# Output norms scaled on VectorE through a PSUM bank, and weight remainders in two pieces, in a two-layer decoder step on one core

## The reference, cut to what matters

```
def rms_norm(x, g):
    y = x * rsqrt(mean(x * x, axis=-1) + EPS)
    return y * g

for i in range(2):
    h = rms_norm(x, norm_mix_pre[i])
    m = conformer_conv(h, ...) if i == 0 else mla(h, c_kv, k_rope, ...)
    x = x + rms_norm(m, norm_mix_post[i])
    h = rms_norm(x, norm_ff_pre[i])
    x = x + rms_norm(square(relu(h @ w_up[i])) @ w_down[i], norm_ff_post[i])
    x = x + sigmoid(x @ ple_gate[i]) * (ple[i] @ ple_proj[i])
```

## Time and profile before

| | us |
|---|---|
| median of 3 runs | 1917.44 |
| lowest and highest | 1915.46, 1927.88 |
| the profiled execution | 1916.53 |
| its span, from the first to the last instruction | 1914.4 |
| mean granted clock of TensorE in it | 0.96 of full |

### The profile page before, as it was taken

The page is one execution under the profiler, slowest core; times in us unless marked ns, Lnnn a source line. Parts: engine busy times, 40 slices in busy tenths (PEclk is TensorE's granted clock), DMA queues, the critical chain, the costliest instruction groups (busy, mean ns, idle before and its releaser), DMA issues.

```text
span 1914.4 us, 33398 instructions
## 1 busy us (share of the span) xinstructions
PE 1782.8 (93%) x12372; PEld 1605.6 (84%) x12372; DVE 920.4 (48%) x2169; ACT 737.9 (39%) x1457; POOL 1013.0 (53%) x737
## 2 busy tenths in 40 slices
PE   7987799989999999979899899999979999999978
PEld 6986799988999989879666465666969999999978
DVE  5896899844223256652444344442252222222383
ACT  5655444454444434432233333332332222223332
POOL 4993899967998975563111000001564555555562
PEclk9998899999999999989899899997979999999989
DMA  7331355533554523123003155555212222222201
GB/s 207 94 101 42 119 177 159 185 111 110 177 154 146 163 88 92 50 50 118 1 1 93 35 165 153 148 164 174 93 45 88 88 88 88 88 73 80 67 23 50
DMA packets 183289, 198.55 MB, mean 104 GB/s; under 512 B 32985, under 2 KB 138035, under 8 KB 183170
## 3 DMA queue, kind: packets, MB, share of 16 engines
q1 hardware_dynamic: 178414, 191.92, 32.4%
q10 hardware_dynamic: 4756, 5.04, 0.8%
HBM read 192.14 MB, written 4.79 MB: 103 GB/s over the span
## 4 chain that ended last, share of the span: by engine, by line
PE 71%; DVE 12%; POOL 10%; issue 3%; ACT 3%; DMA 1%; SPq 0%; ACTq 0%; POOLq 0%; DVEq 0%
PE bank L2340 18%; PE bank L2341 17%; PE bank L2342 17%; POOL WL L1328 6%; PE bank L2906 4%; PE bank L2940 3%; PE bank L2864 3%; DVE X L1657 2%; DVE AL L1625 2%; POOL acc L1354 1%; PE bank L2805 1%; DVE AL L1629 1%; PE bank L2786 1%; ACT WH L661 1%; POOL BL L1421 1%
## 5 line engine op out<-in xcount | busy, mean ns | idle before, releaser
L1328 POOL TENSOR_TENSOR WL<-RAW,WH 128x1024 fp32r<-128x1024 f32 (+1 forms) x281 | 666.2, 2380 | 678.5 <-ACT WH L661 676.7
L2340 PE MATMUL bank<-AH,WH 128*128 128x288 f32 x2112 | 646.0, 306 | 64.5 <-DVE AL L1625 31.3
L2341 PE MATMUL bank<-AL,WH 128*128 128x288 f32 x2112 | 633.6, 300 | 0.0
L2342 PE MATMUL bank<-AH,WL 128*128 128x288 f32 x2112 | 633.2, 300 | 0.0
L2340 PEld LDWEIGHTS bank<-AH,WH 128*128 128x128 f32 x2112 | 407.4, 193 | 80.0 <-DVE AL L1625 33.9
L2341 PEld LDWEIGHTS bank<-AL,WH 128*128 128x128 f32 x2112 | 407.9, 193 | 0.9
L2342 PEld LDWEIGHTS bank<-AH,WL 128*128 128x128 f32 x2112 | 407.3, 193 | 0.0
L661 ACT ACTIVATE WH<-RAW 128x1024 fp32r<-128x1024 f32 (+1 forms) x283 | 293.4, 1044 | 276.7 <-PE bank L2342 271.5
L2340 PE MATMUL bank<-BH,WH 128*128 128x288 f32 (+1 forms) x1120 | 337.7, 302 | 13.3 <-DVE S L1667 7.0
L2341 PE MATMUL bank<-BL,WH 128*128 128x288 f32 (+1 forms) x1120 | 334.8, 299 | 0.0
L2342 PE MATMUL bank<-BH,WL 128*128 128x288 f32 (+1 forms) x1120 | 334.6, 299 | 0.0
(11 more groups left out here) (271 smaller groups left out, 2128.8 us busy)
## 6 DMA issues: line engine op xcount, KB each, us to landing
RAW<-in_w_up SPq DMA_DIRECT2D x48, 1024.0 KB, 5.4
RAW<-in_w_down SPq DMA_DIRECT2D x48, 1024.0 KB, 5.0
RAW<-in_cache_kv_latent SPq DMA_DIRECT2D x128, 256.0 KB, 2.8
RAW<-in_conv_pw SPq DMA_DIRECT2D x16, 512.0 KB, 7.4
RAW<-in_conv_pw SPq DMA_DIRECT2D x8, 1024.0 KB, 5.0
RAW<-in_ple_gate SPq DMA_DIRECT2D x8, 1024.0 KB, 5.0
RAW<-in_cache_k_rope SPq DMA_DIRECT2D x128, 32.0 KB, 2.8
RAW<-in_w_o SPq DMA_DIRECT2D x4, 1024.0 KB, 4.9
```

What stands on the lines that cost most here:

```text
L1328: nc.gpsimd.tensor_tensor(split_part(WL, d, q), raw_part(d, q), split_part(WH, d, q).bitcast(F32), ALU.subtract).then_inc(lo_done, 1)
L2340: nc.tensor.matmul(out, wh, xh, start=first, stop=False)
L2341: nc.tensor.matmul(out, wh, xl, start=False, stop=False)
L2342: return nc.tensor.matmul(out, wl, xh, start=False, stop=last)
```

## The change

Three things change; the opening (everything up to pw2) is as it was, apart from a bank that part of the convolution uses.

1. The POOL scales of y0, m0, y1 and m1 go. The inverse root of a half is written to a PSUM bank (`rstd_row`: bank 4 + h, which held its total; for lv bank 5 − h). DVE multiplies Y by gain and row into another bank (7 for even tiles, 6 or 5 for odd), and adds that to X in a second instruction; `update` makes the first of these two tiles ahead. PE's `total` gets waits, so that it does not write a bank that is still read.
2. 71 parts of weights (the first four slabs of ffa, ffb and mlp1, and all of gate0, dkv, dq, uq, wo, gate1) have their remainder made in two instructions of half the columns.
3. In the last layer the units 0 to 2 and 4 to 6 of the first chunk run by input tile (`up_by_rows`): tile k of three units, then tile k + 1. The second half's total stands after k = 1. ACT and DVE work in an order to match, and POOL's remainders come behind the adds.

```
+SHORT_PARTS = {w for w, (d, q) in enumerate(PART_AT) if DENSE[d][1] in ("gate0", "dkv", "dq", "uq", "wo", "gate1") or
+               DENSE[d][1] in ("ffa", "ffb", "mlp1") and DENSE[d][2] < 4}
...
+        def rstd_row(st, h):
+            return bank[5 - h if st == "lv" else 4 + h][:, 0:H] if st in XS + ["lv"] else R2[:, h, :]
+        def scaled_tile_of(st, h, m):
+            return bank[(5 if (st, h) == ("y0", 0) else 6) if m % 2 else 7][:, 0:H]
...
             def after_mixer(st, v):
...
                     if m == 1:
                         squared(1, 5)
+                    if m == 3:
+                        hi_next()
+                        squared(1, 6)
                     if m == 4:
                         hi_next()
-                        squared(1, 6)
-                hi_next()
-                squared(1, 7)
+                        squared(1, 7)
+                root_of(st, 1)
...
             def lo_part(w):
                 d, q = PART_AT[w]
                 pool.wait_ge(hi_done, w + 1)
-                nc.gpsimd.tensor_tensor(split_part(WL, d, q), raw_part(d, q), split_part(WH, d, q).bitcast(F32),
-                                        ALU.subtract).then_inc(lo_done, 1)
+                dst, src, hi = split_part(WL, d, q), raw_part(d, q), split_part(WH, d, q).bitcast(F32)
+                if w in SHORT_PARTS:
+                    a = part_width(d)[0] // 2
+                    nc.gpsimd.tensor_tensor(dst[:, 0:a], src[:, 0:a], hi[:, 0:a], ALU.subtract)
+                    dst, src, hi = dst[:, a:], src[:, a:], hi[:, a:]
+                nc.gpsimd.tensor_tensor(dst, src, hi, ALU.subtract).then_inc(lo_done, 1)
...
             def after_mixer(st):
...
-                lo_next()
-                add(st, 1, 4)
-                scales(0, 3)
...
-                lo_next()
-                add(st, 1, 7)
-                lo_next()
+                for m in range(4, 8):
+                    lo_next()
+                    add(st, 1, m)
...
-                scales(0, 0, 2)
-                add(st, 1, 2)
...
-                lo_next(3)
-                scales(1, 0, 4)
-                lo_next()
-                scales(1, 4, 8)
-                lo_next(4)
+                for m in range(2, 8):
+                    add(st, 1, m)
+                lo_next(8)
...
             def update(st, h, post, v, first=0, last=KT + 1):
+                def scaled_by_rstd(m):
+                    if m >= 2:
+                        dve.wait_ge(x_done, XU(st, h, m - 2))
+                    nc.vector.scalar_tensor_tensor(out=scaled_tile_of(st, h, m), in0=half(Y, m, h), scalar=gain(post, m),
+                                                   in1=rstd_row(st, h), op0=ALU.mult, op1=ALU.mult).then_inc(y_scaled, 1)
+                if first == 0:
+                    dve.wait_ge(rstd_done, RSTD(st, h))
+                    scaled_by_rstd(0)
+                    scaled_by_rstd(1)
                 for m in range(first, last):
                     if m < KT:
-                        dve.wait_ge(sc_done, SC(st, h, m))
-                        nc.vector.scalar_tensor_tensor(out=half(X, m, h), in0=scaled[:, SC(st, h, m) % 2, :],
-                                                       scalar=gain(post, m), in1=half(X, m, h), op0=ALU.mult,
-                                                       op1=ALU.add).then_inc(x_done, 1)
+                        dve.wait_ge(y_scaled, XU(st, h, m))
+                        nc.vector.tensor_tensor(half(X, m, h), half(X, m, h), scaled_tile_of(st, h, m), ALU.add)\
+                            .then_inc(x_done, 1)
                     if m:
                         lo(v, h, m - 1, half(X, m - 1, h))
+                    if m + 2 < KT:
+                        scaled_by_rstd(m + 2)
...
+                rstd(sty, 1)
+                update(sty, 1, post, v, 0, 1)
                 for c in range(NCH):
                     u_square(c, 0)
                     u_square(c, 1)
-                    if c == 0:
-                        rstd(sty, 1)
                     u_square(c, 2)
                     if c == 0:
-                        update(sty, 1, post, v, 0, 4)
+                        update(sty, 1, post, v, 1, 3)
                     u_square(c, 3)
                     if c == 0:
-                        update(sty, 1, post, v, 4)
+                        update(sty, 1, post, v, 3)
...
+                def up_by_rows(first, units, then=None):
+                    h = first // 4
+                    for k in range(KT):
+                        pe.wait_ge(a_lo, A(f"ff{layer}", h, k))
+                        for n in range(first, first + units):
+                            j, t = n % 4 // 2, n % 2
+                            if k == 0:
+                                ready(d0 + j, t, 0)
+                                pe.wait_ge(bank_free, u0 + n + 1)
+                            ins = three(bank[(u0 + n) % BANKS][:, 0:H], wpart(d0 + j, k, t), rows(Asrc, k, h), k == 0,
+                                        k == KT - 1)
+                            if k == KT - 1:
+                                ins.then_inc(unit_done, 1)
+                        if k == 1 and then:
+                            total(*then)
...
-                up(0, 0, 2)
-                total(sty, 1)
-                up(0, 2, 8)
+                up_by_rows(0, 3, (sty, 1))
+                up(0, 3, 4)
+                up_by_rows(4, 3)
+                up(0, 7, 8)
```

More of the change, by code:

```diff
@@ L1020, in mlp @@
                 for c in range(NCH):
+                    if c == 0:
+                        a_split(sty, f"ff{layer}", 1, 0, 1)
                     relu(c, 0)
@@ L1028, in mlp @@
                     if c == 0:
[L1029 removed]
+                        a_split(sty, f"ff{layer}", 1, 1, 3)
                     relu(c, 3)
@@ L1433, in adds @@
                     add(st, h, m)
-            def scales(st, h, first=0, last=KT):
-                for m in range(first, last):
-                    scale(st, h, m, half(Y, m, h))
             for m in (2, 4, 6):
@@ L1490, in _ @@
                 lo_next()
-            scales("m0", 1)
             def after_mixer(st):
-                def scales(first, last):
-                    for m in range(first, last):
-                        scale(st, 0, m, half(Y, m, 0))
                 for m in range(4):
@@ L1525, in u_split @@
                                             ALU.subtract).then_inc(u_lo, 1)
-                def scales(h, first, last):
-                    for m in range(first, last):
-                        scale(st, h, m, half(Y, m, h))
                 for c in range(NCH):
[L1532 to L1539, removed]
+                    for n in range(3):
+                        u_split(c, n)
                     for p in range(4):
@@ L1727, in conv_late_taps @@
                         else:
-                            run = bank[7][:, 0:TS].rearrange("p (s t) -> p s t", s=NS)
+                            run = bank[6][:, TP - H:H].rearrange("p (s t) -> p s t", s=NS)
                             src = V[:, m, VP:VW].rearrange("p (s c) -> p s c", s=NS)[:, :, c:c + TQ]
@@ L1788, in scaled_tile @@
                     dve.wait_ge(a_lo, A("sw", h, m - 2))
-                nc.vector.tensor_tensor(scaled[:, m % 2, :], half(Y, m, h), R2[:, h, :], ALU.mult).then_inc(z_done, 1)
+                nc.vector.tensor_tensor(scaled[:, m % 2, :], half(Y, m, h), rstd_row("lv", h), ALU.mult)\
+                    .then_inc(z_done, 1)
             def swish_lo(h, m):
@@ L1990, in mlp @@
                 down(last, 1, 6)
+                dve.wait_ge(p_lo, 6 * layer + 6)
                 update(st, 0, post, v, 0, 2)
```

48 lines of the change are left out of this document (16 added, 32 removed).

## The result

The changed kernel took 1904.95 us in the median of six runs (1900.22 to 1905.91), the kernel before 1921.97 in its six (1915.46 to 1927.88): a ratio of 0.9902, with a 95% interval from 0.9878 to 0.9925. (The ratios in this text are estimates over the single runs and differ a little from the quotient of two medians, here 0.9911.) That is about 1% faster, a small gain but clear of the scatter, inside the range (1886 to 1914) and 6 us above the forecast of 1899. The profiled execution took 1904.5 (span 1902.5) against 1916.53.

A forecast was written before the change was run, and what follows sets the result against it. TensorE, busy 93% of the span, was taken to bound the kernel, so only its pauses and clock count. Gains of 18.2 us took the profiled 1916.53 to 1898.3, forecast as 1899 for the median, range 1886 to 1914.

The forecast's parts named there:

- The views: Profile page: PE decides, so gains come from its pauses or clock; the list of waits names the pauses.
- the four rows' 66.4 us: PE waits for AL (31.3), WL (16.1), AL's other form (12.0) and S (7.0): the most the change could touch.
- The tile: Norm updates: DVE's scaled row, add and AL take 1.27 us a tile, bad end 1.48, against 1.41 before.
- AL in turn with pieces: Rival: on four halves with POOL remainders beside the update, a tile takes 1.72, costing 14.4 us: 1913; chance 0.13.
- Places 1 to 3: Layer 0: mixer norm halves gain 0.5 and 0, layer norm 1.1, MLP norm halves 1.7 and 0.8 us.
- the rival of the clock: Six mostly half-clock PE stretches, 28.9 us, stay at full clock as pauses shrink: 10 us more, 1889; chance 0.17.
- The lists: Beside dkv, dq and uq weights POOL is close to late: 0.5 us lost, from 2 lost to 1 gained.
- Place 4: Last layer's mixer norm and first eight units: 8.6 us gained (5 to 13), mostly in the second half.
- The rival of late weights: Last layer: remainders 1 to 3 and first down slabs come no sooner, 8.6 falls away: 1907.6; chance 0.13.
- Place 5: Last layer's MLP norm and gate: shorter waits for embedding copies and a remainder, 6.0 us gained (4 to 8).
- the sum: Whole kernel: 0.5 + 0 + 1.1 + 1.7 + 0.8 − 0.5 + 8.6 + 6.0 = 18.2 us gained over the profiled execution.

The follow-up runs named there:

- a_hold: Changed kernel, POOL held before the second remainder part of latent key slabs 2 and 3 until DVE issued the attention product it met; ratio 0.9878.
- a_hold_again: a_hold, unchanged, run once more for a profile on its slower level; 1899.31 us.
- a_hold_units: a_hold with PE's first chunk of the last layer unit by unit again, the total after the second unit; 1902.22 us, ratio 0.9921.
- a_early: a_hold with ACT's copies of the last layer's third and fourth weight parts moved to after the first and fourth splits of X; 1897.34 us.
- b_collide: Kernel before, DVE's last-block product of heads 2 and 4 made to wait until POOL ended the first remainder part there; 1915.55 us, ratio 0.9991.

## Why the prediction was right, and where it was not

*The views.* The list of waits led to the right places: AL, WL and S fell as named, and the four rows' 66.4 us became 48.3, though most of that went from AL with a gain (31.3 to 17.3), not from the other form (12.0 to 14.2).

*The tile.* 1.27 was taken, 1.22 measured where DVE has only the three instructions of a tile. In the second half of layer 0's mixer norm a copy that the sum left out stands between them, a tile takes 1.58, beyond the bad end of 1.48, and the half lost 1.2. AL in turn with pieces (1.72) did not come. AL does wait for POOL, but only where a remainder happens to lie beside it (1.46 at 1399.29, 0.74 at 1396.14). That rival was priced at 14.4; on its four halves AL took 0.3 us longer than alone in all, and 2.0 in the first half of the last layer's mixer norm.

*Places 1 to 3.* 1.9 against 1.6 for the first two, by luck: the first half of the mixer norm gave 1.4 more than foretold, the second 1.2 less. For the MLP norm of layer 0 5.1 against 2.5: the two waits for remainders at 616 and 647 fell by 1.0 and 1.3, near the 0.6 and 1.1 reckoned, and the half-clock stretches behind them went. That is the rival of the clock, in part: of its six stretches those near 616, 647 and 1835 are gone in the changed kernel, those at 705 and 1855 are half as long, and the one at 424 stays. The 0.8 of that norm's second half did not come: there PE waits for POOL's last add of squares for 2.5 us, where it waited 1.1.

*The lists.* The prediction took 0.5 lost with an end of 2 lost; it was 2.0 in this execution. The profiles of a_hold, a_hold_again, a_hold_units and a_early, which run the same instructions up to there, lose 0.2 to 0.4. So the price was about right, and the 2.0 belongs to the one execution and not to the pieces.

*Place 4.* 9.3 against 8.6, by a way that was half right. The two pauses are the ones named. The first half gave 3.9 where the working had 1.3, since the clock stayed up but for 3.4 us. (The working's own factor does not follow: half of the matmuls at half the clock is 1.5 and not 1.25, which would have put the end of unit 3 at 1415, later than before; the measured factor is nearer 1.1.) The down units gave back 3.2 and not 1.4, and not for their weights, as foretold, but for squares. The rival of late weights did not come: the third remainder came when foretold.

*Place 5.* 6.1 against 6.0: the second of the two waits for embedding copies there, 3.23, is gone, and the remainder's 5.73 are 0.76.

*What failed.* The step "the sum" took a gain of 0 for every stage that the change does not touch. Attention is touched by nothing but the shift in time, and it lost 8.2 us, 6.7 by two lost races and the half clock behind them and 1.4 by half clock at the first head. Without that loss the places give 20.4, and the median would have been near 1897, 2 below the forecast. The time came within 0.3% of the forecast because a loss that was not seen stood against gains that were priced a little low. As a ratio it is closer still, 1899 to 1917.44 being 0.9904 against 0.9902 measured, but that is luck: the median of before had risen by 4.5 us with three more runs. And with the races held off the same change gave 23.3 us in one profiled execution and 17.2 in the other, so the 18.2 foretold is right to within what the clock alone moves from one execution to the next, and no closer.

## What to carry to other kernels

A gain that moves everything behind it also moves every race behind it: look at the untouched stages for instructions of VectorE and GpSimd that start within a fraction of a us of each other, and settle such a race with a wait where it costs nothing, as here (a wait at two places, 6.7 us in the traces). Set two traces side by side matmul by matmul before believing that a sum was right; a sum that fits can be two errors. To scale on VectorE from a PSUM bank, in two instructions instead of one, pays where GpSimd was the other half of the pair.

## What the runs showed of the hardware that was not expected

A product of 128x512 from SBUF to SBUF on VectorE with one SBUF input can be held up by a GpSimd remainder of 128x1024 until that ends, 2.47 to 2.68 us instead of 0.49, and which of the two waits can't be read from their starts: at 0.06 us apart in the trace, VectorE waited once and GpSimd once. The same 89 matmuls took 20.6 us at half clock in the kernel before and 11.7 at the full clock in b_collide, though both have the same pauses, within a tenth of a us, in the 20 us ahead of them. One kernel's runs lie on levels 5 us apart (the changed kernel with the hold) or 11 (b_collide), which is more than most of the steps of this change.
